# Splitting each product of the recurrence's scan into two of 32 stationary columns

## The reference, cut to what matters

```python
def step(S, inp):
    rt, wt, kt, vt, at, bt = inp
    sa = jnp.einsum('bhvk,bhk->bhv', S, at)
    S = S * wt[:, :, None, :] + sa[..., None] * bt[:, :, None, :] + vt[..., None] * kt[:, :, None, :]
    return S, jnp.einsum('bhvk,bhk->bhv', S, rt)
```

## Time and profile before

| | us |
|---|---|
| time, median of three | 2380.37 |
| lowest, highest | 2376.43, 2385.64 |
| span of the profiled execution | 2371.5 |
| scan of layer 0 in that span | 414.2 to 620.0 |
| scan of layer 1 in that span | 1625.5 to 1828.2 |

### The profile page before, as it was taken

How to read it: one execution, slowest core, us unless ns; L and a number is a source line. 1 busy time by engine, 2 the same in 40 slices (tenths; PEclk the granted TensorE clock), 3 DMA queues, 4 the chain that set the end, 5 groups by cost and what they waited for, 6 DMA issues and landing times. The chain is left out here.

```text
span 2371.5 us, 53901 instructions
## 1 busy us (share of the span) xinstructions
PE 2118.4 (89%) x23898; PEld 1360.0 (57%) x23898; DVE 720.8 (30%) x1768; ACT 487.9 (21%) x1120; POOL 275.6 (12%) x463
## 2 busy tenths in 40 slices
PE   6999899899899999999999689998898999986774
PEld 2454443899644444445556465555897887743443
DVE  1033435767431011310000023446775211300001
ACT  2123322333220000301111133323332302110001
POOL 0000000443100001101111200002442000011111
PEclk8999999899999999999999889997999999998886
DMA  7249825000122112639999811110001335799993
GB/s 284 71 156 344 285 93 195 3 4 5 55 89 94 66 66 99 237 104 379 386 384 384 295 53 48 63 49 2 4 4 50 140 133 209 262 380 379 384 382 124
DMA packets 183060, 399.91 MB, mean 169 GB/s; under 512 B 6672, under 2 KB 29072, under 8 KB 182640
## 3 DMA queue, kind: packets, MB, share of 16 engines
q1 hardware_dynamic: 170672, 361.94, 42.4%
q0 software_dynamic: 8576, 23.08, 2.6%
q10 hardware_dynamic: 3648, 12.45, 1.8%
HBM read 365.47 MB, written 31.98 MB: 168 GB/s over the span
## 5 line engine op out<-in xcount | busy, mean ns | idle before, releaser
L493 PE MATMUL ps<-H,memory 128*128 128x512 f32 (+2 forms) x1728 | 616.4, 513 | 12.3 <-DMA memory<-in_w_in 10.5
L493 PEld LDWEIGHTS ps<-H,memory 128*128 128x128 f32 (+1 forms) x1728 | 328.7, 191 | 287.7 <-issue 251.3
L730 PE MATMUL ps<-memory 64*64 64x32 f32 (+2 forms) x10112 | 333.4, 231 | 32.3 <-DVE memory L1623 10.3
L993 PE MATMUL ps<-memory 128*32 128x256 f32 x5120 | 307.5, 403 | 57.8 <-DMA memory<-in_eu 56.3
L730 PEld LDWEIGHTS ps<-memory 64*64 64x64 f32 x10112 | 321.1, 144 | 41.6 <-issue 19.7
L493 PE MATMUL ps<-memory 128*128 128x512 f32 (+3 forms) x928 | 319.8, 496 | 6.8 <-issue 3.0
L993 PEld LDWEIGHTS ps<-memory 128*32 128x32 f32 x5120 | 188.4, 116 | 174.2 <-issue 89.5
L493 PEld LDWEIGHTS ps<-memory 128*128 128x128 f32 (+1 forms) x928 | 173.7, 188 | 145.1 <-issue 127.5
L1018 PE MATMUL ps<-memory 128*32 128x256 f32 x2560 | 144.8, 380 | 4.9 <-ACT memory L1341 3.8
L1913 POOL TENSOR_TENSOR memory<-memory,cons 128x256 f32<-128x256 f32 x160 | 118.0, 753 | 122.8 <-DVE memory L1595 79.9
L1978 POOL DMA_DIRECT2D expert_rows<-memory x128 | 69.5, 543 | 436.9 <-DVE memory L1845 415.2
(11 more groups left out here) (251 smaller groups left out, 1807.1 us busy)
## 6 DMA issues: line engine op xcount, KB each, us to landing
memory<-in_eg SPq DMA_DIRECT2D x32, 2048.0 KB, 18.8
memory<-in_eu SPq DMA_DIRECT2D x32, 2048.0 KB, 24.6
memory<-in_ed SPq DMA_DIRECT2D x32, 2048.0 KB, 21.8
memory<-in_w_ada SPq DMA_DIRECT2D x24, 2048.0 KB, 10.4
memory<-in_w_in SPq DMA_DIRECT2D x20, 2048.0 KB, 8.2
expert_rows<-memory SPq DMA_DIRECT2D x4, 3456.0 KB, 23.6
memory<-in_w_out SPq DMA_DIRECT2D x4, 2048.0 KB, 7.9
memory<-expert_rows ACTq DMA_DIRECT2D x19, 384.0 KB, 6.9
```

The source lines that it names most:

```text
L493: ins = mm(ps[0:M, bank, 0:w], lhs(k), rhs(k), start=(k == 0), stop=(k == n - 1))
L730: ins = mm(out[cols, j], lhs[rows, j, :], rhs[rows, j], start=(n == 0), stop=(n == len(terms) - 1))
L993: ins = mm(out_.rearrange("p (x n) -> p x n", x=2), XGT[:, k, g * GROUP:g * GROUP + GROUP], sets[b][:, 0:2, k * 512 + c * P:k * 512 + c * ...
```

## The change

The helper `heads` cuts the 64 stationary columns of each product into two halves of `HALF = 32`, and issues each half as a product of its own with the whole moving operand. The first half writes to the first 32 of the 64 output partitions and the second half to the other 32. `start` and `stop` are as they were, each half accumulating in its own partitions. The signal still comes from the last product. No other line is touched.

```diff
+HALF = CH // 2
@@ heads
                                 for h in range(2):
-                                    rows, cols = (slice(CH * (h ^ x), CH * (h ^ x) + CH) for x in (held, made))
-                                    ins = mm(out[cols, j], lhs[rows, j, :], rhs[rows, j], start=(n == 0),
-                                             stop=(n == len(terms) - 1))
+                                    rows = slice(CH * (h ^ held), CH * (h ^ held) + CH)
+                                    for c in range(0, CH, HALF):
+                                        cols = slice(CH * (h ^ made) + c, CH * (h ^ made) + c + HALF)
+                                        ins = mm(out[cols, j], lhs[rows, j, c:c + HALF], rhs[rows, j], start=(n == 0),
+                                                 stop=(n == len(terms) - 1))
                                 if signal and j == RJ - 1 and n == len(terms) - 1:
                                     ins.then_inc(sem(signal), 1)
```

## The result

| | before | after |
|---|---|---|
| median us (lowest to highest) | 2380.37 (2376.43 to 2385.64, three runs) | 2672.82 (2668.76 to 2673.71, four runs) |
| ratio, with 95% interval | 1 | 1.1229 (1.1207 to 1.1251) |
| span of the profiled execution | 2371.5 | 2667.0 |
| the two scans in it | 408.5 | 699.2 |
| the rest of the span | 1963.0 | 1967.8 |

A fourth run before took 2416.57 us with the same program and stays out. The change costs 292 us, 12.3%. Nearly all of it lies in the scans: of the 295.5 us that the profiled span grew, 290.7 us are there and 4.8 us in the rest.

A forecast was written before the change was run, and what follows sets the result against it. TensorE was taken to bound the scans, and after the change its instruction fetch: 182 blocks at 3.85 us plus 10 us of waits, 711 us of scan, 302 more, span 2674 us plus 8.9 gives 2683 us, range 2560 to 2770.

The forecast's parts named there:

- Blocks: TensorE instructions in the two scans, in blocks of 256: 92 before, 90 added, 182 after.
- Price of a block: Fetching 256 TensorE instructions in the scans takes 3.85 us whatever the array does; 182 blocks make 701 us.
- the 10 us of waits: Added to the scans for the long waits at each scan's first chunk (3.4 and 3.6 us) and the scans' ends.
- The lower end: A block's fetch costs at least about 3.3 us, from the shortest block (3.29 us, 0.84 us idle); 2581 us in all.
- The row this hung on: Four TensorE stops of 0.76 to 1.53 us inside runs of products, read as waiting for the next 256 instructions.
- The array's term: In the scans, 5120 matmuls with 32 moving columns could start twice as often: at most 73 us less, covered by the fetch.
- The clock: Falls with TensorE idle about half of each block; up to 3.4 us of work, under 3.85, so little is added.
- Rival 1: Column halves on the same rows don't overlap in the scans: 373 us more, 2753 us; chance 0.14 with the slow-issue case.
- The case paired with this rival: Each TensorE instruction takes 16.7 ns to issue: 778 us of scan; shares the chance of 0.14.
- Rival 2: The fetch shortens to 2.4 us a block once it binds: 472 us of scan, 2444 us; chance 0.12 with values up to 2581.
- Rivals 3 and 4: Fetches stay hidden in the scans: loads halve, 2307, rather 2340 us (0.05); or no effect on time, 2380 us (0.03).
- Span and median: The median of the runs was taken to stand 8.9 us above the profiled span: 2674 becomes 2683 us.

The follow-up runs named there:

- e5: Kernel before plus three stretches of small matmuls on constants behind its last result; 28.4 ns a matmul written out, 9.3 ns in a loop.
- e3: Changed kernel with each one-term product also cut into two halves of its moving columns, four pieces in all; 3150.13 us, ratio 1.330 to the kernel before.
- e2: Kernel before with all products split into halves of 32 stationary columns except `join` and `grow`; 2575.90 us, ratio 1.087.
- e6: Changed kernel, but one-term products keep 64 stationary columns and are cut into two halves of their moving columns; 2882.69 us, ratio 1.212 to the kernel before.
- (b): Stretch of e5 added to the kernel before: 256 products split into 32-column halves, in a hardware loop of 16 passes; 9.3 ns a matmul.
- (c): Stretch of e5 added to the kernel before: 128 whole products of 64 stationary and 32 moving columns, in a loop of 16 passes; 29.2 ns a start.
- (a): Stretch of e5 added to the kernel before: 2048 products split into 32-column halves, written out in a row, 32 blocks; 116.4 us, 3.64 us a block.
- e4: Kernel before with four no-operations behind each product of the scan, which didn't reach the program; 2377.59 us, ratio 1.004.

## Why the prediction was right

Forecast 2683 us in 2560 to 2770, slower; measured 2672.82 us.

- **Blocks.** 182 were forecast from 92 packets and 23,040 added instructions. The trace of after has 182.0, and 181 packets.
- **Price of a block.** Forecast 3.85 us, from ends of 3.29 and 4.16; 699.2 / 182 = 3.84 us, waits included. Forecast and measurement differ by the 10 us of waits that I had added, and little else: 711 us of scan against 699.2. The long waits did stay (3.4 and 3.6 us), but they count inside 3.84 us. With nothing else around, a block costs 3.64 us (e5); e3, with smaller pieces, has 3.77. What makes these three differ is open. The mechanism was right; that the time came out within 0.4% is in part luck. 3.85 us was a choice between ends 0.9 us apart, and with e5's 3.64 us the same sum would have given 182 x 3.64 + 10 = 672 us of scan, 2644 us.
- **The lower end.** "At least about 3.3 us" doesn't follow from its row. The 0.84 us of idle time in that block was a wait for VectorE, as at 518.47 us, so the next block was there within 3.29 us and the row sets no lower end. The shortest blocks of the changed kernel last 3.1 us. The line of that wait:

```profile
1750.25 2.97 PE L730 MATMUL ps<-memory 64*64 64x64 f32 x132 [0.84 <-DVE memory L1623]
```

- **The row this hung on.** Four stops in a kernel whose PE is busy for 91% of its scans, three of them at a distance of six times 256 instructions, with one packet of q8 landed before each of the two stops of the earlier trace rows. e5 shows what they were.
- **The array's term.** "At most 73 us less" was a little high and rightly dropped. By e5 two halves save 29.2 - 18.6 = 10.6 ns, 54 us for 5120 matmuls; inside a block of the changed kernel they start only every 12 ns even at full clock ((1.75 - 0.22) / 126). None of it arrives.
- **The clock.** It fell, to 0.69 and 0.66, and added little, as forecast: at the lower level a block of 64-column products took 3.10 us of work in 3.73 us. It raised the work in a block to 445.6 / 182 = 2.4 us on the mean, so PE stands for 36% of a block and not for half. In e2 and e6, where 64 stationary columns meet the lower level, it did cost, and there my expectations were too low by 37 and 120 us of scan. The reason given, that the clock "fell to 0.5 in stretches with idle time", isn't borne out by the kernel before, where PE was busy for 12.01 of 12.50 us at 0.50, nor by e6:

```profile
434.50:447.00 12.50, 12.01 (x270) 11.91 (x272) 6.14 (x19) 2.19 (x8) 2.31 (x4) 0.50 0.01 3
```

- **Rival 1** (halves on the same rows don't overlap) fell with e5: (b) runs both column halves on the same rows and takes 18.6 ns for the two, (c) 29.2 ns for the whole of them; one half after the other would not be faster than (c). Its signs didn't come in the change either: PE has 254 us of gaps, and in the block at 754.64 us the 64-column halves start every 12 ns ((1.76 - 0.22) / 127), not every 29. By the rule of the Trainium skill that the prediction quoted for it ("TensorE: Matmul & The Clock Gate", section "Part 3: Packing small matmuls — row/col tiling"), loads on the same rows wouldn't overlap running matmuls; e5 (b) disagrees for different column groups. The case paired with this rival, 16.7 ns an instruction, fell as well: e5 (b) takes 9.3 ns for two instructions.
- **Rival 2** (the fetch gets shorter once it binds, 2.4 us) fell too: it is 3.84 us, and 3.64 us in e5 (a), where every block stops. The request itself is in no trace; the packet still starts only 1.1 to 1.2 us after a block is entered (for the blocks of 2442.98 and 2446.45 us in e5).
- **Rivals 3 and 4** need hidden fetches. "Runtime: NRT & Kernel Launch", section "Instruction fetch mechanics", of the Trainium skill has them "mostly hidden". For the kernel before the trace agrees, 5 of 408 us; for the changed one it is the bound.
- **Span and median** stand 5.8 us apart after, where I had carried over 8.9.

What stays open: what the 3.6 to 3.8 us are made of. In e5's block of 2442.98 us the packet starts some 1.2 us after the block is entered, takes 0.9 us, and PE goes on 1.4 us after it has landed; no run took these parts further apart. Nor was a loop over the chunks tried. A chunk of the changed kernel is 182 / 16 = 11.4 blocks, some 2900 instructions, nearly three times the loop of 1024 that needed no further packet in e5, so whether such a loop would stay resident no run shows.

## What to carry to other kernels

Count instructions as a resource of their own: 256 of them in a row, written out, cost TensorE 3.6 to 3.8 us here, however little they do. A float32 product is four instructions, so at under 60 ns of array time for each product the fetch is the bound; cutting products finer gained time here only in a loop whose code stayed resident (e5). Look for stops "<-issue" inside a run of matmuls at distances that are multiples of 256 instructions: a few of them say that the kernel is at the edge.

## What the runs showed of the hardware that was not expected

- A hardware loop of 1024 instructions fetched 4 packets in 16 passes and ran at 9.3 ns a matmul with its load (e5). The loop of 512 instructions lost nothing at its turn: 29.2 ns a start through all its passes.
- The clock spent much of the scans at its lower level, though PE never stopped for long: 0.69 and 0.66 on the mean in the change, with some 1.4 us idle in every 3.8 us, and 0.53 and 0.52 in e3. Idle time alone isn't the cause: in e6 it was as low (0.65 and 0.57) with PE idle for 3% of the time, and in e5 (c), with PE busy throughout, it was 1.00. What sets it, the runs don't show.
- `pe.nop(nofuse=True)` left no instruction in the program (e4).
